# Five adaLN weight groups multiplied and summed over rows by VectorE and ScalarE during the input projections, TensorE summing only the 128 partitions

## What is computed

```python
for i in range(4):                                   # layers; mixers: pooling, mLSTM, MLA, pooling
    m = silu(cvec) @ w_ada[i] + b_ada[i]             # (2, 6144): one row for context, one for latents
    mod = m.reshape(2, 6, 1024)                      # shift, scale, gate for mixer; the same for MoE
    h = rmsnorm(x, norm_mix[i]) * (1 + mod[:, 1]) + mod[:, 0]
    y = mixer_i(h)                                   # starts with input projections h @ w_in
    x = x + mod[:, 2] * y
    h = rmsnorm(x, norm_ffn[i]) * (1 + mod[:, 4]) + mod[:, 3]
    x = x + mod[:, 5] * moe(h)                       # 16 experts, 2 of them per token
```

## Time and profile before

| | us |
|---|---|
| median of 3 runs | 1330.68 |
| lowest, highest | 1322.2, 1330.95 |
| the profiled execution's own time | 1324.39 |
| its span, first to last instruction | 1322.7 |

### The profile page before, as it was taken

One profiled execution on the slowest core, in us unless ns is written; L12 is line 12 of the kernel. 1 busy time (PEld: TensorE's weight loads), 2 busy tenths in 40 slices (PEclk: granted clock), 3 DMA queues, 4 the chain that ended last, 5 costly groups with the idle time before them and its releaser, 6 DMA issues.

```text
span 1322.7 us, 24788 instructions
## 1 busy us (share of the span) xinstructions
PE 1200.5 (91%) x10404; PEld 697.5 (53%) x10404; DVE 383.4 (29%) x1218; ACT 316.7 (24%) x716; POOL 122.6 (9%) x188
## 2 busy tenths in 40 slices
PE   4788998789998899899978999999999997789996
PEld 2446544447885554654447643445465444565544
DVE  1345111340004522621132023341451115561113
ACT  1240111231124522211133211230411114401113
POOL 2000100210000000111020000000002111001101
PEclk9898999889999999899989999999999998989998
DMA  9999999794326873898979223891689987658993
GB/s 349 412 421 421 409 413 421 282 350 151 119 96 247 298 314 140 321 409 347 412 271 351 69 96 106 357 363 64 251 344 357 419 359 277 273 214 355 397 390 136
DMA packets 89708, 389.57 MB, mean 295 GB/s; under 512 B 10456, under 2 KB 38604, under 8 KB 53240
## 3 DMA queue, kind: packets, MB, share of 16 engines
q1 hardware_dynamic: 71568, 336.61, 65.2%
q0 software_dynamic: 17456, 51.07, 10.5%
q10 hardware_dynamic: 568, 0.23, 0.1%
HBM read 370.96 MB, written 27.96 MB: 302 GB/s over the span
## 4 chain that ended last, share of the span: by engine, by line
PE 76%; DMA 10%; DVE 5%; SPq 3%; issue 3%; ACT 2%; POOL 1%; POOLq 0%; DVEq 0%; ACTq 0%
PE bank L491 70%; DMA sb_ring<-in_w_ada 3%; PE bank L966 3%; SPq L449 2%; DMA slot_out<-sb_arena,sb_homes 2%; DMA sb_arena<-slot_out,sb_slots 2%; DMA sb_ring<-in_w_exp_up 2%; POOL sb_arena L2132 1%; DVE sb_xT L1994 1%; PE bank L984 1%; DMA slot_out<-sb_arena 1%; DMA sb_arena<-token_rows,sb_rows 1%; PE bank L894 0%; DVE sb_arena L1954 0%; PE bank L1017 0%
## 5 line engine op out<-in xcount | busy, mean ns | idle before, releaser
L491 PE MATMUL bank<-sb_ring,sb_arena 128*32 128x256 f32 (+1 forms) x6112 | 449.9, 429 | 17.3 <-DMA sb_ring<-in_w_exp_down 8.0
L491 PEld LDWEIGHTS bank<-sb_ring,sb_arena 128*32 128x32 f32 x6112 | 212.5, 111 | 197.8 <-issue 108.0
L491 PE MATMUL bank<-sb_arena 128*128 128x128 f32 (+11 forms) x776 | 140.7, 361 | 10.9 <-DVE sb_arena L1840 7.0
L491 PE MATMUL bank<-sb_ring,sb_hT 128*128 128x256 f32 x624 | 140.8, 387 | 6.2 <-ACT sb_hT L1225 6.2
L491 PEld LDWEIGHTS bank<-sb_ring,sb_hT 128*128 128x128 f32 x624 | 120.6, 194 | 26.9 <-issue 9.1
L491 PEld LDWEIGHTS bank<-sb_arena 128*128 128x128 f32 (+2 forms) x776 | 102.7, 194 | 45.6 <-issue 13.0
L491 PE MATMUL bank<-sb_ring,sb_cond 128*2 128x512 f32 x768 | 94.9, 616 | 8.8 <-DMA sb_ring<-in_w_ada 8.5
L491 PE MATMUL bank<-sb_arena,sb_ring 128*128 128x384 f32 (+2 forms) x288 | 95.5, 507 | 3.0 <-DVE sb_arena L1710 2.1
L1941 DVE TENSOR_TENSOR sb_arena<-sb_arena,bank 128x256 f32<-128x256 f32 x40 | 16.8, 421 | 248.9 <-PE bank L491 248.9
L491 PE MATMUL bank<-sb_hT,sb_ring 128*128 128x384 f32 x256 | 85.8, 498 | 2.6 <-ACT sb_hT L1225 2.6
L491 PEld LDWEIGHTS bank<-sb_arena,sb_ring 128*128 128x128 f32 (+1 forms) x288 | 49.9, 181 | 44.9 <-issue 19.0
(11 more groups left out here) (318 smaller groups left out, 1013.8 us busy)
## 6 DMA issues: line engine op xcount, KB each, us to landing
sb_ring<-in_w_ada SPq DMA_DIRECT2D x96, 1024.0 KB, 8.7
sb_ring<-in_w_exp_gate SPq DMA_DIRECT2D x60, 1024.0 KB, 10.4
sb_ring<-in_w_exp_up SPq DMA_DIRECT2D x60, 1024.0 KB, 12.7
sb_ring<-in_w_exp_down SPq DMA_DIRECT2D x60, 1024.0 KB, 15.1
sb_ring<-in_w_mlstm_in SPq DMA_DIRECT2D x12, 1024.0 KB, 12.1
token_rows<-sb_arena POOLq DMA_DIRECT2D x12, 512.0 KB, 7.6
slot_out<-sb_arena POOLq DMA_DIRECT2D x9, 512.0 KB, 8.8
sb_scratch<-in_w_exp_gate SPq DMA_DIRECT2D x4, 1024.0 KB, 9.0
```

Source lines behind the costliest of these rows:

```text
L491: return pe.matmul(out, lhsT, rhs, start=first, stop=last)
```

## The change

Groups 4, 5, 6, 8 and 9 are no longer multiplied by PE. For each of them DVE goes over the 8 row blocks in their ring slots and computes, separately for the context (c = 0) and the latents (c = 1), acc += w[k] * cond[:, k, c], a scalar per partition (`mix`); the first block's c = 0 product is ACT's (`mixed_first`), its c = 1 product a multiplication by DVE. What is left is a sum over the 128 partitions: `ada_sum` runs 8 matmuls with columns of ones and zeros (from `order`) over the two sums of 128 x 2048. The sums lie in memory that is free at the time, for two of the five groups in three pieces.

The units of these groups move into the list between the projection weights, two or three at a time. Groups 4 and 5 are mixed behind `rows_done`, 6 behind the copy of the turned rows, 8 and 9 between DVE's steps of MLA. `ada_sum(4)` stands after the first v result, `ada_sum(5)` after the 18 transposes, `ada_sum(6)` before the first head, `ada_sum(8)` after block 1 of the query expansion, `ada_sum(9)` before attention. Group 10 stays with `ada`, one row block after every second step from step 4. POOL's loads of the tables into `trig`, `rot`, `w_kp` wait for `ada_sum(5)`. In MLA DVE copies the first `positions` before `rope(0)`, where it came after it.

```diff
+        spare = [(trig[:, :, :].rearrange("p a b -> p (a b)"), 1024, 1536), (kpT, 1536, 2048)]
+        in_squares = [[(scratch[:, 0:2048], 0, 2048)], [(scratch[:, 2048:3072], 0, 1024)] + spare]
+        in_heads = [[(view(6156, 2048), 0, 2048)], [(view(8204, 1024), 0, 1024), (view(13512, 1024), 1024, 2048)]]
+        in_keys = [[(view(5568, 2048), 0, 2048)], [(view(7616, 2048), 0, 2048)]]
+        in_latents = [[(hflat[:, 0:2048], 0, 2048)], [(hflat[:, 2048:3072], 0, 1024), (view(0, 1024), 1024, 2048)]]
+        ACC = {4: in_squares, 5: in_squares, 6: in_heads, 8: in_keys, 9: in_latents}
...
-        ADA_MIXER = [(), (4, 5, 6), (8, 9, 10), ()]
+        ADA_MIXER = [(), (), (10,), ()]
...
                 for i in range(4):
                     add((w[:, i * 256:(i + 1) * 256], KC, 256), 2048, (qk_full, 2 * (i + 1)))
+                    if i:
+                        mixed_units(4, *((0, 1), (2, 3, 4), (5, 6))[i - 1])
...
+            def ada_sum(g):
+
+                pe.wait_ge(mrow_ready, g)
+                pe.wait_ge(mod_added, g)
+                pe.wait_ge(acc_mixed, mixed_done[g, KC - 1])
+                for c in range(2):
+                    for q in range(4):
+                        ap, a = [(ap, a) for ap, a, b in ACC[g][c] if a <= q * 512 < b][0]
+                        ins = mm(ps[7][32 * q:32 * q + 2, :], order[:, 4 - c:6 - c], ap[:, q * 512 - a:(q + 1) * 512 - a],
+                                 c == 0, c == 1)
+                ins.then_inc(ada_unit, KC)
...
                         ins.then_inc(v_full, 1)
+                        if c == 0:
+                            ada_sum(4)
+                        if c == 7:
+                            ada_columns(4)
...
-                ins.then_inc(rowc_full, 1)
+                ins.then_inc(turns_full, 1)
+                ada_sum(5)
...
                 maxima_of(0)
-                ada(g4, 0, 1, 2, 3)
+                ada_sum(6)
...
-                        if h % 2 == 0 and c == (2 if h == 0 else 3):
-                            ada(g4 + h // 2, 4, 5)
-                        if h % 2 and c == 0:
-                            ada(g4 + h // 2, 6, 7)
-                        if h % 2 and c == 4:
-                            ada_columns(g4 + h // 2)
-                        if h % 2 and c == 5:
-                            ada(g5 + h // 2, 0, 1)
-                        if h == 2 and c == 0:
-                            ada(g5, 2, 3)
+                        if h == 1 and c == 4:
+                            ada_columns(6)
...
-                ada(g6, 2, 3, 4, 5, 6, 7)
...
-                    ada_beside(ADA_MIXER[2], c)
+                    if c == 1:
+                        ada_columns(9)
+                    if 4 <= c < 20 and c % 2 == 0:
+                        ada(10, (c - 4) // 2)
+                    if c == 21:
+                        ada_columns(10)
...
+            def mixed_first(g):
+
+                i = MIXED.index(g)
+                arrived(act, mixed_unit[g, 0])
+                for ap, a, b in ACC[g][0]:
+                    ins = act.activation(ap, slot(mixed_unit[g, 0])[:, a:b], ACT.Copy, scale=cond[:, 0, 0:1])
+                ins.then_inc(acc_set, 1)
...
+            def mix(g, *rows):
...
+                        for ap, a, b in ACC[g][c]:
+                            if k:
+                                ins = v.scalar_tensor_tensor(out=ap, in0=w[:, a:b], scalar=cond[:, k, c:c + 1], in1=ap,
+                                                             op0=ALU.mult, op1=ALU.add)
+                            else:
+                                ins = v.tensor_scalar(ap, w[:, a:b], cond[:, k, c:c + 1], None, ALU.mult)
+                            ins.then_inc(acc_mixed, 1)
...
                 ins.then_inc(rows_done, 1)
 
-                v.wait_ge(rowc_full, 1)
-                v.tensor_copy(rowc.rearrange("p d k t h -> p (d k t h)"), ps[4][:, 64:136]).then_inc(rowc_set, 1)
+                mix(4, *range(KC))
+                v.wait_ge(ada_unit, 5 * KC)
+                mix(5, *range(KC))
+                mod_columns(4)
+                v.wait_ge(turns_full, 2)
+                v.tensor_copy(rowc.rearrange("p d k t h -> p (d k t h)"), ps[4][:, 64:136]).then_inc(gate_tok, 1)
+                v.wait_ge(out_m, 32)
+                mix(6, *range(KC))
+                mod_columns(5)
```

143 lines of the change are left out of this document (99 added, 44 removed).

## The result

| | before | after |
|---|---|---|
| median, 20 runs each | 1322.7 us | 1329.64 us |
| lowest, highest | 1317.62, 1332.44 | 1325.0, 1337.45 |
| profiled execution, span | 1322.7 | 1327.6 |
| mean granted clock of that execution | 0.962 | 0.943 |

The changed kernel takes 1.005 of the time before, 95% interval 1.0034 to 1.0065: half a per cent slower, +6.9 us between the medians, where -3.6 us (-0.3%) was forecast. It stays within the 1% named in the prediction, but the direction is wrong. The time lies inside the range and 2.5 us above the forecast of 1327.1, and that nearness is luck: the forecast started from 1330.7, the median of three runs of before, and twenty runs put that median at 1322.7. The difference was missed by 10.5 us, and 8.0 of them cancel against the base.

A forecast was written before the change was run, and what follows sets the result against it. PE was taken to bound nearly everything, except chains through ACT and DVE in the heads. Projections +11.7, heads +0.5 and layer 2 -15.8 gave -3.6 us: 1324.4 to 1320.8 profiled, 1327.1 on the median, range 1312 to 1339.

The forecast's parts named there:

- DVE's price: Mixing on DVE: a multiply-add of 2048 elements takes 2.361 us alone, 2.28 in a row of instructions.
- the wait: Layer 1 projections: PE waits 6.3 us (4.1 to 9.9) for DVE at the sum of group 4.
- the clock behind it: Layer 1 projections: PE's clock drops behind the wait at the sum of group 4, costing 1.7 us.
- The rival of no wait: Layer 1 projections: DVE is through before the sum of group 4, so -11.6 in all, 1319 us; chance 0.13.
- that of the slower DVE: Mixing on DVE: multiply-adds take 25% more, sums 4 and 5 wait longer, in all +12, 1342 us; chance 0.16.
- The cover of sum 5: Layer 1 projections: DVE is ready 4 us before PE reaches the sum of group 5, so no wait there.
- The columns of groups 4 and 5: Layer 1: the transposes of a group's columns are as many as before and cancel, as long as nothing waits.
- new drops of the clock: Layer 1 heads: three new drops of PE's clock behind idle time, 1.7 us each, +5.1 (1.7 to 5.1).
- the pairs on the path: Layer 1 heads: removing two pairs inside numerators gives -3.7, the pair ahead of turned head 2 gives -0.9.
- The rival by which the heads give 20 us: Layer 1 heads: PE's pairs delayed the ACT and DVE chain, so 20.2 us come off; -24, 1306 us; chance 0.11.
- In attention: Layer 2: 12 pairs go (-22.0), eight single row blocks stay (+7.3), the columns' wait goes (-1.0).
- I price every new wait of 2 us or more with 1.7 us besides: All stages: each new PE wait of 2 us or more costs 1.7 us of low clock, from rows around a 2.49 us wait.

The follow-up runs named there:

- run 3: Changed kernel with the sum of group 4 behind the third v result instead of the first; ratio 0.9962 to the kernel before.
- second profile of before: Kernel before run again without an edit, on another chip, for a second profiled execution; ratio 0.9992 to the kernel before.
- run 5: Changed kernel with 20 or 28 unused matmuls in four waits of the heads, group 6's rows copied out one head earlier; 0.9971 of the kernel before.
- run 8: Kernel before with layer 2 changed, two pairs of layer 1 moved into waits, 8 unused matmuls ahead of attention; 0.985 of before, 1305.41 us.
- second pair of profiles: Both kernels run again without an edit on another chip: changed kernel 1.0036, kernel before 0.9992, as ratios to the kernel before.
- run 4: Changed kernel with unused matmuls for the heads' waits, all writing the same partitions, 20 taking 13.06 us instead of 3.4; 1.0231 of the kernel before.
- run 10: Changed kernel with shorter filler in the heads, 8 and 16 unused matmuls instead of 20 and 28; 0.9992 of the kernel before.

## Why the prediction was wrong in its sign

**Projections: right in every term that was named.** DVE's price (2.343 against 2.361 us), the wait (6.20 against 6.3), the clock behind it (1.75 us on busy PE against 1.7), no wait at sum 5. The rival of no wait and that of the slower DVE fall with the same rows. The cover of sum 5 was named as 4 us; run 3 shows that it is real and no larger. That the stage came out at 11.70 against 11.7 is partly chance. The columns of groups 4 and 5, 0.9 us (355.08 and 400.19 in PE's timeline), now stand here and left the heads and the output projection; the prediction let them cancel. And a spell behind the norm, which both kernels have, cost 1.1 us more in the first profile of before than in the changed kernel's. Against the second profile of before the stage grew by 12.9.

**Heads: the step that failed.** "Against it stand new drops of the clock: ... 3 x 1.7 = +5.1." The waits were foreseen, at about 6 us, and that the clock would fall behind them, but each was given the price of a wait of 2.49 us. The prediction had five spells in the heads of the changed kernel, two old and three new, 8.5 us. There were four (none behind the 1.80 us at the first head), and they cost 11.15 us by run 5 and 11.6 by the missing clock on busy PE, part of it in the output projection behind them; the two old ones cost 3.4. That is +7.8 to +8.2, not +5.1. With the clock at 1.00 the heads and output projection take 109.4 us (run 5), against 118.7 - 3.4 = 115.3 before, 5.9 less; 0.9 of these are the two groups' columns, so the pairs on the path were worth 5.0, and 4.6 had been put there. Heads with the output projection: +1.8 instead of +0.5. The rival by which the heads give 20 us falls: the chain through ACT and DVE bounds them, as runs 5 and 8 show from both sides.

**Layer 2: right up to attention, 2.5 us short in it.** Up to its ninth sum -1.5 was measured against -2.0. In attention, from the sum's end to the output projection, 81.7 us became 68.5: -13.2 against -15.7. The prediction let the clock there be as before; behind an unchanged wait of 1.43 us 3.4 us were missing (0.34 x 10) instead of 1.7 (0.17 x 10). The changed kernel, and below it before:

```profile
834.00:844.00 10.00, 9.22 (x28) 4.97 (x28) 4.26 (x18) 2.84 (x9) 0.00 (x0) 0.66 0.00 0
```
```profile
818.00:828.00 10.00, 9.02 (x49) 3.27 (x49) 3.50 (x14) 2.08 (x7) 0.00 (x0) 0.83 0.56 197
```

That is 1.7 of the 2.5. The last two steps waited 0.7 us more for DVE and ACT.

**The sum.** +13.5 and -12.9 are +0.7 us, not -3.6, and the two mis-sized prices of the low clock, some 3 us in the heads and 1.7 in attention, are as large as that error of 4.3; against the second pair of profiles +14.9 and -12.5, +2.4. The medians say +6.9 and +5.3. The 3 to 6 us between are in the stages that the change doesn't touch, and in which of the executions were profiled (the changed kernel's second was 4.5 us under its median, that of before 1.3). Nothing here settles them. Over all executions but the fourth run's, the MoE of layer 1 took 174.8 us on the mean behind heads with pairs (5) and 175.8 behind heads without (7), the MoE of layer 2 174.2 behind an attention with pairs (3) and 175.6 behind one without (9), each with a spread of 2 to 5 us; but these means mix chips, and chip by chip the first difference is +1.2, -0.6, +1.5 and 0.0 us. The low clock is large enough to be the whole of it: on busy PE 5.8 and 6.0 us in layer 1's MoE in the two executions of before, 9.2 and 8.0 in those of the changed kernel, and 4.6, 5.8, 6.6 and 5.8 in layer 2's. What would make these spells more or longer was not tried.

**The deciding step** was thus "I price every new wait of 2 us or more with 1.7 us besides", which was taken from two waits of 2.1 and 2.5 us that happened to cost the same. It hid three things: behind the waits of 4 and 5 us in the heads the missing clock was 3.4, 3.4, 3.4 and 5.1 us, behind one and the same wait of 1.43 us it ranged from 0 to 6.8, and waits under 2 us can have one. It accounts for the stages; whether it also accounts for what the medians say beyond them stays open.

The Trainium skill, TensorE: Matmul & The Clock Gate, section "HAM oscillation — how this bites in real kernels", has the price as half of the time that a burst spends at the lower clock. The 3.1 us above follow from the rows in the same way; how long the burst stays there is the other factor, and it was the one that failed.

## What to carry to other kernels

Work on the engine that seems to be the bottleneck may be what keeps its clock up: before taking matmuls out of a wait, price each wait that is left by the spells behind waits of its own length, and where the trace has none, by a range up to its longest spell, not by one shorter example, and read the mean clock beside the time afterwards. Take out only the work that stands between steps without a wait, and move the rest into the waits: run 8, which does that, was at 0.985. Where nothing useful is left, 3.4 to 4.8 us of matmuls into a free bank bought 2.8 us a wait in the heads, and 1.4 us of them kept the clock up ahead of attention; their length must be checked against the wait in the trace, as run 4 was too long and run 10 too short.
